# mLSTM gates and stabiliser as rows on four partitions, gate weights folded onto u, GLA queries zero-padded

## The reference, cut to what matters

```
u = silu(causal_dwconv(cc));  qc = u @ w_mq;  kc = u @ w_mk * HD_C ** -0.5        # per head, 4 heads of 96
gates = concat([qc, kc, v]) @ w_if + b_if                                       # 8 columns a token
ig, lf = gates[:4], log_sigmoid(gates[4:])
Fc = cumsum(lf);  a = Fc + m0                                                   # over the tokens of the block
Dm[t, s] = Fc[t] - Fc[s] + ig[s]  for s <= t
m = max(a, max_s Dm);  w_in = exp(Dm - m);  w_st = exp(a - m)
num = ((qc . kc) * w_in) @ v + w_st * (qc @ C0);  den = sum((qc . kc) * w_in) + w_st * (qc . n0)
h = num / max(|den|, exp(-m))
C1, n1 = exp(a_L - m_L) * (C0, n0) + sum_s exp(Dm[L, s] - m_L) * kc[s] (v[s], 1);  m0 <- m_L
```

## Time and profile before

| | us |
|---|---|
| median of three runs | 1419.49 |
| lowest to highest | 1418.19 to 1437.57 |
| the profiled execution | 1428.77 |
| its span, first to last instruction | 1427.0 |
| PE busy in the span | 1230.1 (86%) |
| DVE busy | 766.3 (54%) |
| ACT busy | 385.5 (27%) |
| POOL busy | 404.2 (28%) |
| mean granted clock of PE | 0.884 |

### The profile page before, as it was taken

One profiled execution on the slowest core, in us unless ns is written; L12 is line 12 of the kernel. 1 busy time (PEld: TensorE's weight loads), 2 busy tenths in 40 slices (PEclk: granted clock), 3 DMA queues, 4 the chain that ended last, 5 costly groups with the idle time before them and its releaser, 6 DMA issues. The chain is left out here.

```text
span 1427.0 us, 15702 instructions
## 1 busy us (share of the span) xinstructions
PE 1230.1 (86%) x5629; PEld 787.1 (55%) x5629; DVE 766.3 (54%) x1795; ACT 385.5 (27%) x771; POOL 404.2 (28%) x421
## 2 busy tenths in 40 slices
PE   5899899999999999999999999979861999999700
PEld 2566475665665665665665454447421777777500
DVE  0024223677777888899889788952422010110088
ACT  1142431433423323422531431142100211112111
POOL 5112115124036036026205501210103100001788
PEclk9999999999999999999999797955775999999955
DMA  8974863654545444444343333320001998889163
GB/s 257 299 235 149 320 180 125 184 156 157 139 147 159 149 138 153 120 154 157 95 135 103 108 115 103 95 76 15 15 16 48 364 371 315 282 310 319 64 235 129
DMA packets 147520, 238.72 MB, mean 167 GB/s; under 512 B 16907, under 2 KB 119234, under 8 KB 147442
## 3 DMA queue, kind: packets, MB, share of 16 engines
q1 hardware_dynamic: 134370, 199.76, 44.0%
q0 software_dynamic: 9008, 29.16, 5.9%
q10 hardware_dynamic: 4064, 8.78, 1.6%
HBM read 211.38 MB, written 26.29 MB: 167 GB/s over the span
## 5 line engine op out<-in xcount | busy, mean ns | idle before, releaser
L1188 PE MATMUL bank_pair<-win,xT 128*128 128x384 f32 (+7 forms) x1152 | 453.0, 545 | 12.8 <-DMA win<-in_w_in 11.6
L1188 PEld LDWEIGHTS bank_pair<-win,xT 128*128 128x128 f32 (+1 forms) x1152 | 214.1, 194 | 192.0 <-issue 104.6
L897 DVE MAX8 top<-score 128x8 f32<-128x384 f32 (+6 forms) x201 | 174.9, 870 | 4.0
L898 DVE MATCH_REPLACE8 score<-top,score 128x384 f32<-128x384 f32 (+6 forms) x201 | 171.9, 855 | 0.0
L1282 PE MATMUL bank_pair<-w_out,yT 128*128 128x512 f32 (+1 forms) x288 | 131.2, 610 | 0.4 <-ACT yT L623 0.4
L567 POOL TENSOR_TENSOR small<-small,pexp 128x4 f32<-128x4 f32 (+1 forms) x9 | 9.4, 1049 | 333.7 <-DVE small L1078 333.7
L1282 PEld LDWEIGHTS bank_pair<-w_out,yT 128*128 128x128 f32 (+1 forms) x288 | 52.4, 185 | 73.8 <-issue 72.0
L1661 DVE TENSOR_TENSOR hT<-gate,bank_pair 128x160 f32<-128x160 f32 x32 | 10.3, 321 | 139.8 <-ACT gate L1609 139.8
L1142 PE MATMUL bank_pair<-ident,lm 128*128 128x128 f32 (+2 forms) x234 | 43.7, 315 | 45.2 <-ACT lm L733 15.2
L1564 POOL DMA_INDIRECT xg<-x_rows,ids x16 | 15.0, 938 | 183.0 <-PE bank_pair L1679 182.4
L918 DVE CUSTOM_DVE_ANT_0 lm<-bank_pair,score 128x128 f32<-128x128 f32 (+8 forms) x36 | 26.0, 723 | 73.6 <-PE bank_pair L1225 51.1
(11 more groups left out here) (345 smaller groups left out, 2000.2 us busy)
## 6 DMA issues: line engine op xcount, KB each, us to landing
win<-in_w_in SPq DMA_DIRECT2D x90, 768.0 KB, 4.5
win<-in_w_in SPq DMA_DIRECT2D x18, 1024.0 KB, 5.4
win<-in_w_in SPq DMA_DIRECT2D x18, 840.0 KB, 5.4
win<-in_w_in SPq DMA_DIRECT2D x18, 800.0 KB, 4.7
wg<-in_w_exp_gate SPq DMA_DIRECT2D x12, 1024.0 KB, 6.9
wu<-in_w_exp_up SPq DMA_DIRECT2D x12, 1024.0 KB, 11.4
wd<-in_w_exp_down SPq DMA_DIRECT2D x12, 1024.0 KB, 13.0
expert_rows<-rows ACTq DMA_DIRECT2D x16, 512.0 KB, 8.0
```

Source lines behind the costliest of these rows:

```text
L897: step(V.max(top8[0:n], sc))
L898: step(V.match_replace(sc, top8[0:n], sc, NEG))
L1188: last = mmul(zb[0:n, 0:w], xT[:, kk, 0:n], win[:, i % NWIN, k, 0:w], start=(kk == 0), stop=(kk == KD - 1))
```

## The change

The gates are computed with the gate columns on partitions, `[4 input gates at 0, 4 forget gates at GROW = 32]` by 128 tokens, from eight matmuls over `uT` and the values. For that, at tile 0, PE transposes `wmq` and `wmk` and multiplies them by `w_if` (16 matmuls), and ACT lays the result into `wug`. The log sigmoid, the running sum, the running maximum and m are then rows on four partitions: two scans there in slot 7 in place of four on 128 partitions in slot 8. `rows3` holds three sets of rows (g = ig - F, the state's factor, exp(-m)); one transpose in slot 10 turns them into columns `cols3`. Only the running maximum is spread to 128 partitions (slot 9). The product of the queries with the carried state is made by itself in slot 11 and multiplied by the state's factor as ACT copies it out to `inter`; the numerator is added to it by DVE. GLA's queries lie in `qz`, each head on its 64 partitions with zeros on the other 64, so scores and output use 128 partitions and need no wait between heads. Three memsets (`wug`, `qz`, `rows3`) are added at the start, the bias is loaded by two DMAs onto four partitions each, and m is loaded and stored as `[4, 1]`. The core of the diff, ACT first, then DVE, then PE:

```diff
@@ -759,6 +772,17 @@
 if s == 0:
...
+    if t == 0:
+        act.wait_ge(S("consts"), 1)
+        act.wait_ge(S("wT_ps"), 1)
+        copy(mw[0:HC, :, 0:HC], h4(RA, HC, HC))
+        A.mul(mp[0:HC, :, 0:HC], h4(RB, HC, HC), HC ** -0.5).then_inc(S("wT_ready"), 1)
+        act.wait_ge(S("wu_ps"), 1)
+        for k in range(2):
+            g0 = GROW * k
+            copy(wug[:, 0:H, g0:g0 + H], RA[0:HC, 0:2 * H * H].rearrange("p (h g) -> p h g", h=H)[:, :, H * k:H * k + H])
+            last = copy(wug[:, H:2 * H, g0:g0 + H], wif[:, 2 * H:3 * H, H * k:H * k + H])
+        last.then_inc(S("wu_ready"), 1)
@@ -802,31 +826,36 @@
 if s == 6:
...
-    copy(qkT[:, :, 0:n], h4(RA, 128, n)).then_inc(S("qkT_ready"), 1)
+    for b in range(2):
+        copy(qz[64 * b:64 * b + 64, b:H:2, 0:n], h4(RA, 128, n)[64 * b:64 * b + 64, 0:2])
+    copy(kgT[:, :, 0:n], h4(RA, 128, n)[:, 2:4]).then_inc(S("qkT_ready"), 1)
...
-    step(A.activation(sm(n, LNT, H), sm(n, LNT, H), ACT.Exp))
-    A.activation(sm(n, LNT, H), sm(n, LNT, H), ACT.Ln, bias=1.0).then_inc(S("ml_ln"), 1)
-if s == 7:
-    act.wait_ge(S("irow_ps"), t + 1)
-    copy(mi[:, :, 0:n], h4(RB, 128, n)).then_inc(S("irow_ready"), 1)
+    step(A.activation(lf[:, 1, 0:n], lf[:, 1, 0:n], ACT.Exp))
+    A.activation(lf[:, 1, 0:n], lf[:, 1, 0:n], ACT.Ln, bias=1.0).then_inc(S("ml_ln"), 1)
+if s == 8:
+    if t == NPT:
+        act.wait_ge(S("states_loaded"), 16 * N_STATE)
+    act.wait_ge(S("mm_ready"), t + 1)
+    A.activation(rows3[GROW:GROW + H, 0:n], maxrow[:, 0:n], ACT.Exp, bias=m0t[:], scale=-1.0)
+    act.wait_ge(S("m_ready"), t + 1)
+    A.activation(rows3[2 * GROW:2 * GROW + H, 0:n], mrow[:, 0:n], ACT.Exp, scale=-1.0).then_inc(S("rows_ready"), 1)
 if s == 9:
...
-    act.wait_ge(S("fm_ready"), t + 1)
-    if t == NPT:
-        act.wait_ge(S("states_loaded"), 16 * N_STATE)
+if s == 10:
+    act.wait_ge(S("cols_ps"), t + 1)
+    copy(cols3[0:n], RA[0:n, 408:408 + 3 * GROW]).then_inc(S("cols_ready"), 1)
+if s == 11:
+    act.wait_ge(S("inter_ps"), t + 1)
...
-        last = A.activation(mi[:, h, 0:n], mw[:, h, 0:n], ACT.Exp, bias=m0t[:, h:h + 1])
-    last.then_inc(S("wst_ready"), 1)
-if s == 11:
-    act.wait_ge(S("cols_ps"), t + 1)
-    act.wait_ge(S("gi_ready"), t + 1)
-    A.activation(sm(n, EM, H), RA[0:n, 4:8], ACT.Exp, scale=-1.0).then_inc(S("mcol_exp"), 1)
+        A.activation(inter[0:n, h, :], RA[0:n, (HC + 1) * h:(HC + 1) * (h + 1)], ACT.Copy, scale=cols3[0:n, GROW + h:GROW + h + 1])
+    copy(carry[:], RA[0:HC, 400:400 + H]).then_inc(S("inter_ready"), 1)
...
-    A.activation(mw[0:n, :, 0:n], mw[0:n, :, 0:n], ACT.Exp).then_inc(S("w_ready"), 1)
+    A.activation(mw[0:n, :, 0:n], mw[0:n, :, 0:n], ACT.Exp, scale=-1.0).then_inc(S("w_ready"), 1)
 if s == 13:
@@ -1046,13 +1075,21 @@
 if s == 6:
...
-    step(TT(sm(n, GATES, 8), RB[0:n, 0:8], bif[0:n], ALU.add))
-    step(TS(sm(n, LF, H), sm(n, GATES + H, H), 0.0, None, ALU.min))
-    STT(out=sm(n, LNT, H), in0=sm(n, LF, H), scalar=2.0, in1=sm(n, GATES + H, H), op0=ALU.mult,
+    fps = RB[GROW:GROW + H, 0:n]
+    TS(lf[:, 0, 0:n], fps, bif[GROW:GROW + H, :], 0.0, ALU.add, ALU.min)
+    step(TS(lf[:, 1, 0:n], fps, bif[GROW:GROW + H, :], None, ALU.add))
+    STT(out=lf[:, 1, 0:n], in0=lf[:, 0, 0:n], scalar=2.0, in1=lf[:, 1, 0:n], op0=ALU.mult,
...
+if s == 7:
+    if t == NPT:
+        dve.wait_ge(S("states_loaded"), 16 * N_STATE)
...
-    TT(sm(n, LF, H), sm(n, LF, H), sm(n, LNT, H), ALU.subtract).then_inc(S("lf_ready"), 1)
-if s == 7:
+    step(TT(lf[:, 0, 0:n], lf[:, 0, 0:n], lf[:, 1, 0:n], ALU.subtract))
+    step(V.tensor_tensor_scan(frow[:, 0:n], ones[0:H, 0:n], lf[:, 0, 0:n], 0.0, ALU.mult, ALU.add))
+    step(STT(out=rows3[0:H, 0:n], in0=RB[0:H, 0:n], scalar=bif[0:H, :], in1=frow[:, 0:n], op0=ALU.add, op1=ALU.subtract))
+    tell(V.tensor_tensor_scan(maxrow[:, 0:n], rows3[0:H, 0:n], rows3[0:H, 0:n], m0[g][:], ALU.max, ALU.max), "mm_ready", t + 1)
+    TT(mrow[:, 0:n], maxrow[:, 0:n], frow[:, 0:n], ALU.add).then_inc(S("m_ready"), 1)
@@ -1062,16 +1099,7 @@
-    dve.wait_ge(S("irow_ready"), t + 1)
-    dve.wait_ge(S("lfrow_ps"), t + 1)
-    for h in range(H):
-        ins = V.tensor_tensor_scan(mm[:, h, 0:n], h4(RB, 128, n)[:, h], mi[:, h, 0:n], m0[g][:, h:h + 1], ALU.add, ALU.max)
-    tell(ins, "mm_ready", t + 1)
 if s == 9:
-    dve.wait_ge(S("frow_ps"), t + 1)
-    tell(TT(mw[:, :, 0:n], h4(RB, 128, n), mm[:, :, 0:n], ALU.subtract), "fm_ready", t + 1)
@@ -1082,37 +1110,36 @@
 if s == 11:
...
-    dve.wait_ge(S("cols_ps"), t + 1)
-    tell(TT(sm(n, GI, H), sm(n, GATES, H), RA[0:n, 0:4], ALU.subtract), "gi_ready", t + 1)
-    dve.wait_ge(S("wst_ready"), t + 1)
+    dve.wait_ge(S("mb_ps"), t + 1)
+    dve.wait_ge(S("cols_ready"), t + 1)
...
-        ins = STT(out=mw[0:n, h, 0:n], in0=mw[0:n, h, 0:n], scalar=sm(n, GI + h), in1=minmask[0:n, 0:n],
-                  op0=ALU.add, op1=ALU.min)
+        ins = STT(out=mw[0:n, h, 0:n], in0=RB[0:n, 128 * h:128 * h + n], scalar=cols3[0:n, h:h + 1], in1=latemask[0:n, 0:n],
+                  op0=ALU.subtract, op1=ALU.max)
...
 if s == 12:
...
-    TT(qcT[:, :, 0:n], qcT[:, :, 0:n], mi[0:HC, :, 0:n], ALU.mult).then_inc(S("qs_ready"), 1)
...
 if s == 13:
...
-    num = RA[0:n, 0:H * (HC + 1)].rearrange("p (h d) -> p h d", h=H)
+    num = inter[0:n]
...
-    dve.wait_ge(S("mcol_exp"), t + 1)
+    dve.wait_ge(S("inter_ready"), t + 1)
...
+    tell(TT(num, num, RA[0:n, 0:H * (HC + 1)].rearrange("p (h d) -> p h d", h=H), ALU.add), "num_ready", t + 1)
...
-    step(TT(sm(n, DEN, H), sm(n, DEN, H), sm(n, EM, H), ALU.max))
+    step(TT(sm(n, DEN, H), sm(n, DEN, H), cols3[0:n, 2 * GROW:2 * GROW + H], ALU.max))
...
-    step(TT(cS[g][:], cS[g][:], mi[0:HC, :, n - 1:n].to_broadcast([HC, H, HC + 1]), ALU.mult))
-    V.tensor_copy(m0[g][:], mm[:, :, n - 1])
+    step(TT(cS[g][:], cS[g][:], carry[:].unsqueeze(2).to_broadcast([HC, H, HC + 1]), ALU.mult))
+    V.tensor_copy(m0[g][:], mrow[:, n - 1:n])
...
 if s == 14:
@@ -1319,11 +1346,22 @@
+for h in range(H):
+    tr(RA[0:HC, 128 * h:128 * h + HC], wmq[:, h, :])
+    last = tr(RB[0:HC, 128 * h:128 * h + HC], wmk[:, h, :])
+last.then_inc(S("wT_ps"), 1)
+pe.wait_ge(S("wT_ready"), 1)
+for h in range(H):
+    mmul(RA[0:HC, 2 * H * h:2 * H * h + 2 * H], mw[0:HC, h, 0:HC], wif[:, h, :], start=True, stop=False)
+    last = mmul(RA[0:HC, 2 * H * h:2 * H * h + 2 * H], mp[0:HC, h, 0:HC], wif[:, H + h, :], start=False, stop=True)
+last.then_inc(S("wu_ps"), 1)
+pe.wait_ge(S("wu_ready"), 1)
...
-pe.wait_ge(S("hs_ready"), t)
+pe.wait_ge(S("num_ready"), t)
@@ -1371,24 +1409,16 @@
-    srcs = [qcT, kcT, mp]
-    for b in range(3 * H):
-        last = mmul(RB[0:n, 0:8], srcs[b // H][0:HC, b % H, 0:n], wif[:, b, :], start=(b == 0), stop=(b == 3 * H - 1))
+    srcs = [uT, mp]
+    for b in range(2 * H):
+        last = mmul(RB[0:GROW + H, 0:n], wug[:, b, :], srcs[b // H][0:HC, b % H, 0:n], start=(b == 0), stop=(b == 2 * H - 1))
...
 if s == 7:
...
-    for h in (0, 2, 1, 3):
-        b = 64 * (h % 2)
-        if h == 1:
-            step(last)
-        last = mmul(RA[0:n, 128 * h:128 * h + n], qkT[b:b + 64, 2 + h // 2, 0:n], qkT[b:b + 64, h // 2, 0:n], start=True, stop=True)
+    for h in range(H):
+        last = mmul(RA[0:n, 128 * h:128 * h + n], kgT[:, h // 2, 0:n], qz[:, h, 0:n], start=True, stop=True)
...
-    done("ml_nabs")
-    for h in range(H):
-        last = mmul(RB[:, 128 * h:128 * h + n], sm(n, GATES + h).to_broadcast([n, 128]), ident[0:n, 0:n], start=True, stop=True)
-    last.then_inc(S("irow_ps"), 1)
 if s == 8:
@@ -1397,53 +1427,41 @@
-    done("lf_ready")
-    done("irow_ready")
-    for h in range(H):
-        last = mmul(RB[:, 128 * h:128 * h + n], sm(n, LF + h).to_broadcast([n, 128]), ident[0:n, 0:n], start=True, stop=True)
-    last.then_inc(S("lfrow_ps"), 1)
 if s == 9:
...
-        last = mmul(RB[:, 128 * h:128 * h + n], sm(n, LF + h).to_broadcast([n, 128]), upper[0:n, 0:n], start=True, stop=True)
-    last.then_inc(S("frow_ps"), 1)
+        last = mmul(RB[0:n, 128 * h:128 * h + n], ident[0:H, h:h + 1].to_broadcast([H, n]), maxrow[:, 0:n], start=True, stop=True)
+    last.then_inc(S("mb_ps"), 1)
...
-    for h in (0, 2, 1, 3):
-        b = 64 * (h % 2)
-        if h == 1 or (n < 128 and h):
-            step(last)
+    for h in range(H):
...
-        if n < 128 and b:
-            step(last)
-        last = mmul(RA[0:n, DV * h:DV * h + DV], qkT[b:b + 64, h // 2, 0:n], gS2[b:b + 64, h // 2, :], start=False, stop=True)
+        last = mmul(RA[0:n, DV * h:DV * h + DV], qz[:, h, 0:n], gS2[:, h // 2, :], start=False, stop=True)
...
+if s == 10:
+    done("yb_normed")
+    done("rows_ready")
+    tr(RA[0:n, 408:408 + 3 * GROW], rows3[:, 0:n]).then_inc(S("cols_ps"), 1)
 if s == 11:
-    done("yb_normed")
-    mmul(RA[0:n, 0:4], upper[0:n, 0:n], sm(n, LF, H), start=True, stop=True)
+    done("cols_ready")
...
-        last = mmul(RA[0:n, 4 + h:5 + h], mm[0:1, h, 0:n], ones[0:1, 0:1], start=True, stop=True)
-    last.then_inc(S("cols_ps"), 1)
```

(15 more changed lines are left out.)

37 lines of the change are left out of this document (24 added, 13 removed).

## The result

The changed kernel takes 1381.7 us (median of four runs, 1378.3 to 1387.1) against 1425.0 for the kernel before in the same set (1418.2 to 1437.6): 0.969 of it, 95% interval 0.961 to 0.977, so 3.1% faster. The forecast was 1378 in 1357 to 1401. The spans of the two profiled executions are 1427.0 and 1385.3 us, 41.7 apart, where the sum said 41.

The account below looks back on a forecast made before the run. PE bounds tiles 0 to 4, VectorE's path tiles 5 to 7. Tiles 1 to 4 22, tile 0 0.5, tiles 5 to 7 12, short tile 5.5, clock 4, new waits -3: 41 us, giving 1378, range 1357 to 1401.

Parts of the forecast that it names:

- PE by the count of records: PE in each tile: short matmuls cost by record count, not columns; 12.89 us out, 7.41 in, 5.5 us gained.
- VectorE's operations: VectorE in tile 6: gate operations move to four partitions; 8.5 us out, 3.9 in, net 4.6 us.
- I take 4.5 for tiles 5 and 6: VectorE's gain in tiles 5 and 6, 4.5 us each; 2.6 in tile 6 if L1094's hold moves on.
- rival 1: VectorE is the wall earlier, from tile 4 or even 3: 26 us gained, 1393 us; chance 0.17.
- a microsecond of PE is worth a microsecond in tiles 0 to 4: Tiles 0 to 4: PE is the wall, so its saving of 5.5 us a tile counts in full.
- Tiles 5 to 7: VectorE's own path counts there: 4.5 us for tiles 5 and 6 each, 3 for tile 7, 12 together.
- New waits: PE in slot 10 waits for the normed GLA output where VectorE is late: 3 us lost, bounds 0 and 8.
- Tile 0 and the fold: Folding the gate weights before the recurrence costs 5 us, 4 to 8; tile 0 nets 5.5 - 5 = 0.5.
- The short tile: The 32-token tile: row copies, GLA output and gates save 7.0 us, 1.5 comes back, 5.5 gained.
- The clock: Clock falls at the gates in tiles 0, 3 and 4: 4 us comes back, at most 6.8, possibly 0.
- Three falls stand at one and the same line: Reason given for taking 4 us of clock: falls in tiles 0, 3 and 4 during or right behind the gates.
- Rival 4: VectorE's rows on four partitions cost about 1.2 us each, not 0.34: 31 us slower, 1450; chance 0.03.

Follow-up runs that it names:

- e4: The kernel before with half of VectorE's selection rounds (16 in place of 32 a tile): 1387.9 us, 0.976 of the kernel before.
- e5: The changed kernel with half of VectorE's selection rounds (16 in place of 32 a tile): 1328.7 us, 0.934 of the kernel before.
- e7: The changed kernel with ScalarE scaling the keys and the state's decay and update as four operations reading PSUM: 1369.1 us, 0.963 of the kernel before.
- e6: The changed kernel with the rows' transpose in slot 11, not 10, and the state's product in 12, not 11: 1379.5 us, 0.967 of the kernel before.
- e11: The changed kernel with e7's edit, e6's edit and the fold moved into tile 0's projection, plus one selection round moved from slot 7 to 0: 1352.4 us.
- e3: The kernel before with its 24 gate records made 128 columns wide, only the first 8 used: 1428.4 us, 0.999 of the kernel before.

## Why the prediction was right, and where its terms were not

- **PE by the count of records: right.** Tiles 1 to 3, where PE is the wall, give 16.6 us for 16.5. The 16 new gate records cost about 0.11 each. Two small misses cancel in this: in tile 3 the new parts take 7.8 us and not 7.41 (the row copy 1.08 for 0.89), so the count gives 5.1 us a tile, and 3.4 us less of low clock in the three tiles, worth 1.7, make up for it. e4 and e5 show the gain in the late tiles too, once VectorE is out of the way.
- **VectorE's operations: right in price, wrong in what they gave.** The new ones sum to 3.3 us (six at 0.28 to 0.34, scans of 0.41 and 0.47, an addition of 0.56) for 3.9. Of the 4.6 for tile 6, 1.9 were busy time and 2.7 a wait; busy time fell by 1.1, and though that wait went, idle time only by 0.9 (14.8 to 13.9). The failed step is "I take 4.5 for tiles 5 and 6": the lower bound beside it, that the hold on L1094 moves on to the keys' scaling, was the case. L1094 stood 1.9 us over the 0.69 that it takes in tile 7, L1123 stands 1.4 over its 0.55. The state's decay is held as well, but that is no second move of the same hold: before, GpSimd's multiplication by the norm's weight (L513) began as the decay ended and held the copy behind it, L1115, 1.21 us where it takes 0.17 in tile 0; now it begins just ahead of the decay and holds that for 1.0. The sum left L1115 out. So the time held in tile 6 went only from 3.0 to 2.4 us. Tile 6 gained 2.0 where the bound said 2.6. e7 takes the held operations out and gets 5.3 us in that tile, most of it clock. The Trainium skill, SBUF — State Buffer, section Who interferes with whom, says that a VectorE instruction with two inputs in SBUF contends with a GpSimd instruction that reads SBUF, and that one with at most one SBUF input does not, outside the two-port modes; the rows of L1122 and L1123 agree, 0.69 and 1.93 us beside the same GpSimd instruction. The copy L1115, with a single input, was held all the same; in which mode it ran, no row shows.
- **Tile 4: rival 1.** The step "a microsecond of PE is worth a microsecond in tiles 0 to 4" fails at tile 4: 5.5 expected, 1.4 measured, PE idle 4.4 us where it was 2.1. Busy shares of 98% for PE and 85% for VectorE did not show that VectorE, once PE was 5 us shorter, would be late at the GLA state (0.38 us), the normed output (1.00) and the tile's end (1.95 for 0.48). Low clock took a part too: 9.4 us in this tile for 6.8, worth 1.3.
- **Tiles 5 to 7: right as a sum (12.1 for 12), not in its parts.** 3.3, 2.0 and 6.9 for 4.5, 4.5 and 3. Tile 7 gained most, and not by waits: PE's busy time fell by 8.0 us there (120.17 in the earlier trace rows to 112.16), of which 6.8 us less of low clock are worth 3.4, and its idle time rose by 1.1. The wait of 3.42 us for VectorE's scans (L1410) went, but one of 3.00 for the GLA state came in the same slot.
- **New waits: the right one named, and too few.** The slot 10 wait costs 3.6 us over tiles 0 to 7 for 3 forecast, and taking it away gives at most that (e6). The larger one, 7.2 us for the GLA state over tiles 4 to 7, stands in slot 9, where the chain of scans now lies in front of VectorE's slot 8; 5.0 us of waits for the scans went from that slot, so 2.2 are new. I costed that chain only for the masking of the scores, and the old wait not at all. That VectorE's order makes this wait is shown by e11: with one round less in slot 7 it goes from tiles 4 to 6.
- **Tile 0 and the fold.** The fold's own 3.9 us is nearly the 5 taken, and with the low stretch behind it dearer in this profile. Tile 0 gained 3.6 us more than forecast: a wait of PE for the scaled keys is gone, 2.67 us in the kernel before, and 3.4 us of low clock, worth 1.7. That wait is the hold again, as that kernel's timeline shows:

```profile
129.75 2.67 POOL L465 TENSOR_TENSOR x<-x,ln0b 128x1024 f32<-128x1024 f32 x1
...
130.74 2.09 DVE L1097 TENSOR_TENSOR kc<-kc,mw 128x384 f32<-128x384 f32 x1
...
132.89 0.53 PE L1445 MATMUL bank_pair<-zm,mp 128*128 128x97 f32 x1 [2.67 <-DVE kc L1097]
```

- **The short tile.** 3.9 us are gained up to the numerator (78.3 to 74.4 us from the tile's start); the rest of the 5.5 lies in the numerator, behind which PE waits for GpSimd's normalisation anyway, 4.58 us before and 6.25 after. That wait is the one that the forecast overlooked. Of this 3.5 us are left when the sample's output projection starts, and 2.1 when it ends: its 32 records have 2.9 us of low clock before and 5.8 after. Before, then after:

```profile
1051.58 15.35 PE L1282 MATMUL bank_pair<-w_out,yT 128*32 128x512 f32 x32 [0.37 <-ACT yT L623]
1010.72 16.76 PE L1309 MATMUL bank_pair<-w_out,yT 128*32 128x512 f32 x32 [0.37 <-ACT yT L636]
```

- **The clock: half right in cause, wrong in place.** Time in low clock falls from 331 to 307 us over the span, at half speed worth 12. In tiles 0 to 4, where PE is the wall and where the three falls of the forecast stand, it goes from 37.5 to 33.3, worth 2. In the experts it is 5.7 less, worth 3, and in tiles 5 to 7 15.6 less (73.8 to 58.2), worth up to 8; the sum had nothing for either. "Three falls stand at one and the same line" did point to the narrow gates, and e3 bears that out. The Trainium skill's rule of the idle array (TensorE: Matmul & The Clock Gate, Part 1) does not explain these falls, since PE was busy in all of them and ahead of them. But e3 also shows that wide gates alone bring nothing back. It took the padding too, and the forecast treated that as a matter of waits only. New low stretches, of 6.8 us at 238.2 and 432.8, stand at the tile boundaries of the changed kernel, behind the router's product of 16 columns; whether that product makes them is not shown.
- **Rival 4** is excluded by L1079 and L1088: 0.28 to 0.34 us, no hold on any of the rows.

The total came out by luck, because misses cancelled: the start with tile 0, and the experts, gave 9 us more than forecast, tile 4 and the short tile 7.5 less.

## What to carry to other kernels

Short records cost their count here, and the count held wherever the engine was the wall; check with the other engine made lighter where that is, because two busy shares do not tell it. A hold between VectorE and GpSimd is not removed with the operation that shows it: look which operation with two operands in SBUF, or which copy, comes under the same GpSimd instruction next. Where the clock falls at one sparse place, look for the next sparse place before counting it as won.

## What the runs showed of the hardware

- In tile 0 low clock moved by 16 us, from the gates to the GLA output, when only the gates were made wide (98.8 in the earlier trace rows, 114.9 in e3), and in tiles 0 to 4 it left both places when both were changed (37.5 to 17.1 us).
- VectorE's operation with two operands in SBUF ended 0.43 us after GpSimd's (736.81 and 736.38), one reading PSUM ran beside it at its usual 0.69. A copy of four columns is held too: 1.21 us beside GpSimd's L513 in tile 6 before, ending 0.03 us after it (783.96 and 783.93), and 0.17 alone in tile 0.
- The start of the recurrence scatters between profiles of unchanged code before it: 75.5, 75.0, 74.2, 73.2 and 71.8 us in the five that begin as the kernel before does. A change of 2 us in that stretch is not told by one profile.
